# A transformer trunk on one core: first feed-forward weights fetched in the stage before it and split in halves, its first transposes over more PSUM banks, pooling bands and norm loads moved later

## The reference

```python
for layer in range(2):
    if layer == 0: mix = attn_recurrent_mixer(h, ...) # ends in  o @ w_out
    else:          mix = multiscale_pool(h, ...)      # windows 2, 4, 8, 16
    h = layer_norm(ALPHA * h + mix, ln_mix_g[layer], ln_mix_b[layer])
    h = layer_norm(ALPHA * h + swiglu(h, w_gate[layer], w_up[layer], w_down[layer]),
                   ln_ffn_g[layer], ln_ffn_b[layer])

def swiglu(h, w_gate, w_up, w_down):
    return (jax.nn.silu(h @ w_gate) * (h @ w_up)) @ w_down
```

## Time and profile before

| | |
|---|---|
| median of 3 runs (lowest to highest) | 2737.99 us (2735.99 to 2739.49) |
| the profiled execution: its time / its span | 2737.52 / 2735.8 us |
| PE busy | 2602.8 us, 95% of the span |
| POOL, DVE, ACT busy | 1077.6, 1292.4, 843.7 us |
| mean granted clock of TensorE | 0.96 of full |
| start of trunk (first transpose) | 1047.47 us into the span |

### The profile page before, as it was taken

How to read it: one execution, slowest core, us unless ns; L and a number is a source line. 1 busy time by engine, 2 the same in 40 slices (tenths; PEclk the granted TensorE clock), 3 DMA queues, 4 the chain that set the end, 5 groups by cost and what they waited for, 6 DMA issues and landing times.

```text
span 2735.8 us, 36593 instructions
## 1 busy us (share of the span) xinstructions
PE 2602.8 (95%) x14303; PEld 2217.5 (81%) x14303; DVE 1292.4 (47%) x2469; ACT 843.7 (31%) x1385; POOL 1077.6 (39%) x638
## 2 busy tenths in 40 slices
PE   7899999699999987999999999999999999999996
PEld 6789999668778876889888777888878788888885
DVE  6789995878776431333333332332322332232224
ACT  3674221333333222322222322322323232332221
POOL 1432222655444423443333433444434344445442
PEclk9999999689999998999999998999999999999998
DMA  3101220323322243232323322233323233333431
GB/s 129 32 17 58 91 74 13 100 85 105 93 85 91 72 142 116 70 93 78 101 71 92 93 75 79 77 99 101 92 62 93 64 90 108 93 94 107 119 105 47
DMA packets 276470, 232.96 MB, mean 85 GB/s; under 512 B 10448, under 2 KB 257296, under 8 KB 276304
## 3 DMA queue, kind: packets, MB, share of 16 engines
q1 hardware_dynamic: 268112, 222.13, 27.3%
q10 hardware_dynamic: 8192, 8.52, 0.9%
HBM read 217.91 MB, written 12.71 MB: 84 GB/s over the span
## 4 chain that ended last, share of the span: by engine, by line
PE 58%; DMA 1%; POOL 1%; ACT 1%; DVE 1%; issue 0%; POOLq 0%; SPq 0%; ACTq 0%; DVEq 0%
PE banks L1819 34%; PE banks L1835 19%; PE banks L1852 1%; PE banks L1857 1%; PE banks L1869 1%; DMA draw<-in_w_down 1%; PE banks L1543 1%; POOL wL L1738 1%; POOL dL L1745 0%; DMA raw<-in_w_up 0%; ACT wH L1913 0%; ACT dH L1919 0%; DVE y L2019 0%; DVE y L1521 0%; PE banks L1854 0%
## 5 line engine op out<-in xcount | busy, mean ns | idle before, releaser
L1738 POOL TENSOR_TENSOR wL<-raw,wH 128x2048 fp32r<-128x2048 f32 x88 | 406.3, 4617 | 596.2 <-ACT wH L1913 596.2
L1819 PE MATMUL banks<-hL,wH 128*128 128x512 f32 (+1 forms) x1760 | 620.4, 352 | 15.9 <-ACT hid L1928 13.5
L1819 PE MATMUL banks<-hH,wL 128*128 128x512 f32 (+1 forms) x1760 | 619.4, 352 | 0.0
L1819 PE MATMUL banks<-hH,wH 128*128 128x512 f32 (+1 forms) x1760 | 617.2, 351 | 0.0
L1999 DVE TENSOR_TENSOR hid<-hid,banks 128x512 f32<-128x512 f32 (+1 forms) x110 | 64.3, 585 | 759.6 <-PE banks L1819 654.8
L1819 PEld LDWEIGHTS banks<-hL,wH 128*128 128x128 f32 x1760 | 332.8, 189 | 65.4 <-ACT hid L1928 15.1
L1819 PEld LDWEIGHTS banks<-hH,wL 128*128 128x128 f32 x1760 | 332.7, 189 | 46.3
L1819 PEld LDWEIGHTS banks<-hH,wH 128*128 128x128 f32 x1760 | 333.2, 189 | 45.0
L1745 POOL TENSOR_TENSOR dL<-draw,dH 128x1024 fp32r<-128x1024 f32 x88 | 220.9, 2510 | 371.9 <-ACT dH L1919 371.8
L2019 DVE TENSOR_TENSOR y<-y,banks 128x512 f32<-128x512 f32 (+1 forms) x340 | 233.1, 686 | 219.8 <-PE banks L1835 218.8
L1835 PE MATMUL banks<-dH,hidL 128*128 128x512 f32 (+1 forms) x748 | 303.9, 406 | 2.3 <-issue 2.3
(11 more groups left out here) (235 smaller groups left out, 4316.4 us busy)
## 6 DMA issues: line engine op xcount, KB each, us to landing
raw<-in_w_gate SPq DMA_DIRECT2D x88, 512.0 KB, 4.7
raw<-in_w_up SPq DMA_DIRECT2D x88, 512.0 KB, 6.1
draw<-in_w_down SPq DMA_DIRECT2D x88, 512.0 KB, 3.5
w_out_part<-in_w_out SPq DMA_DIRECT2D x64, 512.0 KB, 4.0
va<-in_w_in SPq DMA_DIRECT2D x10, 1024.0 KB, 5.4
va<-in_x SPq DMA_DIRECT2D x8, 512.0 KB, 4.9
vg_scratch<-y ACTq DMA_DIRECT2D x32, 128.0 KB, 1.7
y<-in_x SPq DMA_DIRECT2D x8, 512.0 KB, 7.6
```

Source lines behind the costliest of these rows:

```text
L1738: nc.gpsimd.tensor_tensor(wL[:, ff % 2, :, :, :].rearrange("p g k f -> p (g k f)"), raw[:, :, :, :].rearrange("p g k f -> p (g k f)"), wH[ ...
L1819: last = nc.tensor.matmul(banks[:, GU + (2 * q + g) % 3, 0:n], wt[:, ff % 2, g, k, :], h[:, k, a:a + n], start=(k == 0 and part == 0), sto ...
```

## The change

Six edits, all near the border between mixers and trunk.

1. `raw` and `draw` are now memory of the top level, laid over `cqT` and `score_last` of the stages before (they show as `cq_raw` and `last_draw`). SP issues the loads of the first gate and up tile at step (8,2) of mixers and of the first w_down rows at (9,3); it waits for all three at the end of mixers.
2. Tile 7's quarters 2 and 3 are computed from `wq_last`, so that the last two refills of `w_out_part` (4 DMAs of 512 KB) fall away. `wq_last` is laid so that quarters 2 and 3 come first (in `kaT`); tile 8 takes its quarters in the order 2, 3, 0, 1.
3. The first feed-forward tile is split in halves, gate and up, on ACT and on POOL, with ACT's gate half ahead of all copies of `hH`. A later tile is handled whole, as before.
4. The ten first half tiles that are transposed use banks 6, 7, 3, 4, 5, 2, 6, 7, 3, 4 in place of 6 and 7 in turn.
5. SP issues the norm's gain and bias after pair 0's loads, and the pooling weights and scale after pair 2's, in place of ahead of all pairs.
6. POOL builds one window's bands in each of pairs 3 to 6, and scales the pooling weights in pair 8, in place of all in pair 0.

```diff
+    LAST_ORDER = (2, 3, 0, 1)
+    def kept_quarter(t, q):
+        return t == NT - 1 or (t == NT - 2 and q in LAST_ORDER[0:2])
...
             if m == NT and h in (0, 2):
-                for q in (h, h + 1):
+                for q in LAST_ORDER[h:h + 2]:
                     sp.dma_start(wq_last[q], w_v[:, :, q * QW:(q + 1) * QW]).then_inc(wl_loaded[q], 16)
             if out_job(m, h):
                 t, q = out_job(m, h)
-                if 4 * t + q + 1 < 4 * (NT - 1):
+                if t < NT - 1 and 4 * t + q + 1 < 4 * (NT - 1) - 2:
                     load_w(4 * t + q + 1)
+            if (m, h) == (NT - 1, 2):
+                sp.wait_ge(shared_psum, nth["qa", NT - 1])
+                for part, name in enumerate(("w_gate", "w_up")):
+                    sp.dma_start(raw[:, part, :, :], ...).then_inc(ahead_loaded, 16)
+            if (m, h) == (NT, 3):
+                sp.wait_ge(nmax_tail, A_HEADS)
+                sp.dma_start(draw, ins["w_down"][0][0:P, :]).then_inc(ahead_loaded, 16)
+        sp.wait_ge(ahead_loaded, 48)
...
-                if m == NT - 1:
+                if kept_quarter(m, q):
                     w = wq_last[q][:, k, :]
...
+                   first_banks=(PB, PB + 1, DN, DN + 1, DN + 2, GU + 2, PB, PB + 1, DN, DN + 1))
...
-        load_w(0)
         load_w(1)
-        load_d(0)
-        n0.load(...); w_pool and pool_scale loads
+            if g == 0: n0.load(...)
+            if g == 2: w_pool and pool_scale loads
...
+            if ff == 0:
+                for part in range(2):
+                    pool.wait_ge(w_hi, part + 1)
+                    nc.gpsimd.tensor_tensor(wL[:, 0, part, :, :], raw[:, part, :, :], wH[:, 0, part, :, :]...)
+                return
...
-            if g == 0:
-                bands()
+            if g in BANDS_AT:          # {3: 0, 4: 1, 5: 2, 6: 3}
+                bands(BANDS_AT[g])
+            if g == SCALE_AT:          # 8: the two scalings of the pooling weights
...
+        nc.scalar.activation(wH[:, 0, 0, :, :], raw[:, 0, :, :], ACT.Copy).then_inc(w_hi, 1)
-        for j in range(3):
+        for j in range(2):
             n0.high(act, j)
-        high_w(0)
-        for j in range(3, FIRST):
+        nc.scalar.activation(wH[:, 0, 1, :, :], raw[:, 1, :, :], ACT.Copy).then_inc(w_hi, 1)
+        for j in range(2, FIRST):
             n0.high(act, j)
         high_w(1)
```

More of the change, by code:

```diff
@@ L109, in build @@
         y = sb(top, "y", [P, NT, D])
+        cq_raw = sb(top, "cq_raw", [P, QC * L])
+        last_draw = sb(top, "last_draw", [P, L])
+        cqT = cq_raw[:, :].rearrange("p (k t) -> p k t", k=QC)
+        raw = cq_raw[:, 0:2 * DC * P].rearrange("p (g k f) -> p g k f", g=2, k=DC)
+        draw = last_draw[:, 0:D]
         with ExitStack() as heads:
@@ L120, in build @@
                 with stage() as c:
-                    mixers(nc, c, sem, sb, banks, ident, x, meta, ins, score, cqT, kaT, va, y, qz_dram, vg_dram)
+                    mixers(nc, c, sem, sb, banks, ident, x, meta, ins, score, cqT, kaT, va, y, qz_dram, vg_dram, raw, draw)
             hH = sb(top, "hH", [P, DC, L], F32R)
@@ L124, in build @@
         with stage() as c:
-            trunk(nc, c, sem, sb, banks, ident, ins, y, hH, hL, out)
+            trunk(nc, c, sem, sb, banks, ident, ins, y, hH, hL, raw, draw, out)
 def projection(nc, c, sem, sb, banks, ident, x, meta, w_in_v, ins, score, cqT, kaT, va, y, qz_dram, vg_dram):
@@ L646, in _, with mixers @@
             nc.vector.tensor_scalar(at, at, TAKEN_BELOW, MASKED, ALU.is_ge, ALU.mult).then_inc(mask_done, 1)
-def mixers(nc, c, sem, sb, banks, ident, x, meta, ins, score, cqT, kaT, va, y, qz_dram, vg_dram):
+def mixers(nc, c, sem, sb, banks, ident, x, meta, ins, score, cqT, kaT, va, y, qz_dram, vg_dram, raw, draw):
     W = 4 * P
@@ L749, in out_job @@
         jobs = {7: (m - 1, 0), 1: (m - 2, 1), 3: (m - 2, 2), 5: (m - 2, 3)}
-        return jobs[h] if h in jobs and 0 <= jobs[h][0] < NT else None
+        if h not in jobs or not 0 <= jobs[h][0] < NT:
+            return None
+        t, q = jobs[h]
+        return (t, LAST_ORDER[q]) if t == NT - 1 else (t, q)
+    def kept_quarter(t, q):
+        return t == NT - 1 or (t == NT - 2 and q in LAST_ORDER[0:2])
     def norm_tile(m, h, lag):
@@ L1380, in out_added @@
             else:
-                bank, done, signal = q, (op_psum, q + 1), op_added
+                bank, done, signal = q, (op_psum, LAST_ORDER.index(q) + 1), op_added
             at = y[0:n, m, q * QW:(q + 1) * QW]
@@ L1440, with __init__ @@
 class NormSteps:
-    def __init__(self, nc, c, sem, sb, banks, ident, tag, y, tiles, t_banks=(), split=None, like=None, loads=(0,), before=0):
+    def __init__(self, nc, c, sem, sb, banks, ident, tag, y, tiles, t_banks=(), split=None, like=None, loads=(0,), before=0,
+                 first_banks=()):
         self.nc, self.banks, self.ident, self.y, self.tiles, self.t_banks, self.split = (
             nc, banks, ident, y, tiles, t_banks, split)
-        self.loads, self.before = loads, before
+        self.loads, self.before, self.first_banks = loads, before, first_banks
         if like:
@@ L1529, in bank_of, with bank_used @@
     def bank_of(self, i):
-        return self.t_banks[i % len(self.t_banks)]
+        return self.first_banks[i] if i < len(self.first_banks) else self.t_banks[i % len(self.t_banks)]
+    def bank_used(self, i):
+        return max((k for k in range(i) if self.bank_of(k) == self.bank_of(i)), default=None)
     def turn(self, pe, j):
@@ L1538, in turn @@
             i = 2 * j + q
[L1539 to L1540 removed]
+            if self.bank_used(i) is not None:
+                pe.wait_ge(self.lo, self.bank_used(i) + 1)
             for k in range(4):
@@ L1592, in phases, with trunk @@
     return out
-def trunk(nc, c, sem, sb, banks, ident, ins, y, hH, hL, out):
+def trunk(nc, c, sem, sb, banks, ident, ins, y, hH, hL, raw, draw, out):
     NW = len(POOL_WINDOWS)
@@ L1605, in trunk @@
     BW = 528
-    raw = sb(c, "raw", [P, 2, DC, P])
     wH = sb(c, "wH", [P, 2, 2, DC, P], F32R)
     wL = sb(c, "wL", [P, 2, 2, DC, P], F32R)
-    draw = sb(c, "draw", [P, D])
     dH = sb(c, "dH", [P, 2, D], F32R)
@@ new lines, in _, with bands @@
+        made_count = [0]
+        def bands(g):
+            win = POOL_WINDOWS[g]
+            for mat, r, base in ((band, slice(0, P), 0), (edge, slice(0, N_META), N_META), (edge, slice(P - TAIL, P), TAIL)):
+                at = mat[r, g, :]
+                nc.gpsimd.memset(at, 1.0 / win).then_inc(made, 1)
+                made_count[0] += 1
+                pool.wait_ge(made, made_count[0])
+                nc.gpsimd.affine_select(out=at, in_=at, compare_op=ALU.is_gt, fill=0.0, base=win - base,
+                                        pattern=[[-1, P]], channel_multiplier=1).then_inc(made, 1)
+                made_count[0] += 1
+                pool.wait_ge(made, made_count[0])
+                if base == 0:
+                    nc.gpsimd.affine_select(out=at, in_=at, compare_op=ALU.is_ge, fill=0.0, base=0,
+                                            pattern=[[1, P]], channel_multiplier=-1).then_inc(made, 1)
+                    made_count[0] += 1
+                    pool.wait_ge(made, made_count[0])
+                    nc.gpsimd.tensor_tensor(at, at, ident[:, :], ALU.subtract).then_inc(made_all, 1)
```

83 lines of the change are left out of this document (36 added, 47 removed).

## The result

| | before | changed |
|---|---|---|
| median, us (lowest to highest; runs) | 2737.99 (2735.99 to 2740.5; 5) | 2722.53 (2720.63 to 2729.56; 5) |
| the profiled execution: its time / its span | 2737.52 / 2735.8 | 2721.79 / 2720.1 |
| mean granted clock | 0.96 | 0.963 |

The ratio is 0.9949, with a 95% interval of 0.9935 to 0.9963: 14 us faster (10 to 18). The forecast was 2724.0.

The account below looks back on a forecast made before the run. PE was taken to bound the kernel, busy 2602.8 of 2735.8 us, so only its idle time could be had. 2737.5 - 7.0 - 6.8 = 2723.7, stated as 2724.0 since the median is 0.5 above the profiled execution; range 2720 to 2731.5.

Parts of the forecast that it names:

- The mixers' end: End of mixers: tile 7's quarters no longer wait for refilled weights, quarter 3 ends at 1022.7 instead of 1029.69; gain 7.0 us.
- the lower bound of 5.4: End of mixers: the gain in us if quarter 3 took 5.29 us again.
- The opening: Start of trunk: next weight load issued earlier and landing faster; gain 6.8 us, between 5.8 and 7.8.
- 1.0 us of a shorter load: Start of trunk: next load has the queues for itself, 5.24 us instead of 6.28; gain 1.0 us.
- My lower bound, 5.8: Start of trunk: the opening's gain in us if the next load doesn't get shorter.
- gate_up(0): Start of trunk: first gate_up starts 7 to 8.5 us behind the first transpose, against 12.6 before.
- The stall: Trunk's opening: PE's long wait for silu stays at 9 to 12 us, only moved earlier, ending near +40.2.
- The moved POOL work: Pairs 0, 3 to 6 and 8: moving bands and scaling costs nothing; up to 15.8 us without cover.
- That only one gain comes: Mixers' end and trunk's opening: only one of the two gains arrives, time 2731; chance 0.17.
- That both are lost further on: Behind the opening, for instance at phase 1's start: both stalls come back, time 2734 to 2741; chance 0.07.
- The fourth, that more is gained: Trunk's long stall and gate_up(0): PE's clock stays up, 2.7 us gained in each, time 2718.6; chance 0.09.
- The third, the moved work on the pairs' chain: Five pairs: POOL's moved 15.8 us delays PE, doubled with DVE held, time 2755.6, slower; chance 0.03.

Follow-up runs that it names:

- 2: Changed kernel with the refills of w_out_part and tile 8's quarter order 0, 1, 2, 3 restored; 2728.87 us, ratio 0.9967.
- experiment 12: The kernel before, nothing altered, run and profiled again; 2737.8 us, ratio 1.0008 to before.
- experiment 5: Changed kernel with the first feed-forward tile's weights split whole on ACT and POOL, not in halves; 2729.13 us, ratio 0.9968.
- experiment 6: Changed kernel with the ten first half tiles transposed through two banks again; 2724.49 us, ratio 0.9946.
- experiment 4: Changed kernel with pair 0 reordered: w_down's first rows split early, its second rows loaded before the third weights, tile 1's silus before those weights; 2719.7 us, ratio 0.9938.
- experiment 9: Changed kernel with w_down's rows first in pair 0, plus ACT's copies of third and fourth weights put inside the preceding tile's silu steps; 2709.25 us, ratio 0.9896.
- experiment 3: Changed kernel with POOL's bands and scaling, and their loads, back in pair 0; 2724.46 us, ratio 0.9948 to before.
- experiment 7: Changed kernel with all four windows' bands and the scaling, POOL's moved work, in pair 3; 2729.29 us, ratio 0.997 to before.
- experiment 10: The changed kernel, nothing altered, run and profiled again; 2720.54 us, ratio 0.9941 to before.
- Experiment 1: Kernel before with only tile 7's quarters 2 and 3 taken from kaT and the last two refills dropped; 2730.6 us, ratio 0.9969.
- 11: Changed kernel with odd and even feed-forward tiles' weight columns swapped behind the first, computing something else; 2721.09 us, one run.
- 8: Changed kernel with gain, bias, pooling weights and scale issued right behind trunk's first load again; 2726.07 us, ratio 0.9954.

## Why the prediction was right

**The mixers' end: 7.0, measured 6.91.** Every step of it held. Quarter 3 was forecast for 1019.0; it started at 1020.67, and without the 1.64 us by which this execution was late that is 1019.03. It took 3.72 us and not 5.29, so the gain isn't the lower bound of 5.4, and what released it was the copy of the transposes, as said. Kernels with edit 2 gave 34.41 to 34.44 from attention's last matmuls to T, those without it (before, 2, 12) 41.30 to 41.43.

**The opening: 6.8, measured 5.76 (5.93 against experiment 12).** This is the term that was mis-sized. It was made of 5.8 us of earlier issue and 1.0 us of a shorter load. The issue came 5.99 us earlier, and 4.8 of that is the halves' (experiment 5). The load did not get shorter: 6.36 us against 6.28. The step that failed is "it also has the queues for itself: 6.28 against the 5.24 of the load after it, which was alone". I took two loads of one trace, the first with company and the second without, and put their whole difference down to the company. The load after it takes 5.1 to 5.3 us in every kernel here, also where the first one is alone and takes 6.3, so most of the difference isn't the company behind, which is worth 0.5 at most. My lower bound, 5.8, said what would be left without it.

**gate_up(0)** was to start at +7 to +8.5 and started at +5.88, for 40 transposes took 5.95 us: I had carried 1.97 us for eight of them over from the earlier trace rows, where the bank's pauses stand between. At that pace they would have taken 8.5; in the window from 1042 to 1048 us the granted clock was 0.72, between the levels of 1.2 and 2.4 GHz, so a part of them ran at the upper one. It is off the path, as experiment 6 shows, so nothing came of it but a new wait of 2.2 us for the first silu, off the path as well.

**The stall** of 9 to 12 us stayed, 10.66, ending at T + 41.28 where +40.2 was forecast, 1.0 late by the missing term. That it is the order on SP, ACT and POOL, and not the amount of work, is shown by experiments 4 and 9.

**The moved POOL work: 0**, by experiment 3, and 1 to 2 us in the trace if all of it stands in pair 3 (experiment 7, whose median is 5 us worse than that).

**The number.** The two terms gave 12.7 us (12.8 against experiment 12) where 13.8 were forecast, yet the medians are 15.5 apart, 16.3 in experiment 10. That 2722.53 lies below 2724.0, and not a microsecond above it, is luck: the forecast had no term for the clock's changes between executions, which gave 4.35 us in the profiled pair. How much of the medians' difference is theirs no trace tells, as each kernel has one or two. The forecast's own sum, 2737.5 - 13.8 + 0.5, also gives 2724.2 and not 2724.0.

**DVE beside POOL.** DVE's `hidL` of 264 columns took 2.38 us at 1060.21, beside POOL's `wL` (1057.71 to 1062.30), and 0.43 at 1065.06 with POOL idle. The Trainium skill ("SBUF — State Buffer", "Who interferes with whom") has it that a VectorE instruction with two SBUF inputs contends with a GpSimd instruction that reads SBUF. The trace agrees: the first ends 0.29 us behind `wL`.

**The rivals.** That only one gain comes is refuted by experiments 1 and 2. That both are lost further on is refuted by the table: from S to the long silu the difference is 0.45, and from phase 1's transposes to the end 0.13. The fourth, that more is gained as the clock keeps up, wasn't seen where it was put: 24 matmuls behind the stall took 4.90 us against 5.34, which is 0.4. The third, the moved work on the pairs' chain, is refuted by experiment 3 for the change as it stands.

## What to carry over

When a chain has a load in it, don't take the load's gain from the difference of two loads in one trace before other pairs of loads have shown that difference too; 1.0 of 13.8 us was lost in this way, and a look at the loads of the following pairs (6.2, 5.2, 6.2, 5.2), and at what SP issued just ahead of each, would have told. A step brought forward by splitting (gate and up in halves) pays by what it releases next, here the single buffer, and not by the matmuls that it lets start: 4.2 us of earlier gate_up(0) were worth nothing. And a stall that a change leaves where it is deserves its own question: which instruction, ready earlier, stands behind one that waits; here an order that puts a copy of 1.9 us into ACT's pause, and w_down's rows first, gave 11 us more, beside the 16 of the change itself on the same chip.

## What the runs showed of the hardware

- **Time that the clock takes.** PE does the same work from the long silu to phase 1's transposes in all kernels and is busy throughout. It took 283.2 us (changed, 2, 10, 11), 284.6 to 284.7 (1, 5, 7, 9, 12), 286.1 to 286.2 (3, 6, 8) or 287.6 (before, 4). In these four groups TensorE's granted clock was at the lower of its two levels (1.2 and 2.4 GHz) for 27.3, 30.7, 34.1 and 37.6 us of the stretch, the same in all members of a group, so the clock accounts for the difference. It fell four times in each execution, each time at or before the end of a run of the pooling's matmuls of 128 columns; in the changed kernel the first run goes from 1549.74 to 1557.33 and the clock fell at 1554.93, while PE had no gap. Experiment 1's long end is of the same kind: 52.8 us at the lower level from phase 1's transposes on, where the others have 45.1 to 45.9. How long the clock stays down differs between executions of one program: the kernel before has 37.6 and 30.7 us, the changed one 27.3 twice. Whether a program leans to one isn't settled by so few executions. Two spans should therefore be compared stretch by stretch.
- **A load ahead costs 1 us, a load behind nearly nothing.** 512 KB issued 0.4 to 0.8 us behind another 512 KB land after 6.2 us, alone after 5.2 to 5.3 (medians of each of fourteen traces). 2.5 MB queued right behind a load cost it 0.5 us at most, and 512 KB queued 0.7 us behind one cost it nothing or little (5.30 in experiment 9, 5.58 in experiment 4).
- **DVE beside POOL.** DVE's subtraction of 264 columns took 0.43 us, and 2.3 to 2.4 beside a subtraction of 2048 columns on POOL.
